# Two experts' rows gathered and transposed at once; own buffers for a mixer's first two weight blocks; the router's block ahead in the queue

## The chip, the core and the metric

One core of a Trainium2 chip. The metric is the device time in microseconds of one execution. The core has TensorE (PE: matmuls and transposes), VectorE (DVE), ScalarE (ACT), GpSimd (POOL) and SyncE (SP), and 16 DMA engines that move data between the chip's memory (HBM) and on-chip memory. The engines run their own instruction streams in order and wait for each other through semaphores.

## What is computed

One sequence of 512 tokens of width 1024, float32, passes through two blocks. The first is a feed-forward network, a mixer with two kinds of attention, and another feed-forward network. The second is a mixer and a layer of experts, one of which each token picks in a hierarchy:

```python
def first_block(x, ...):
    x = x + 0.5 * swiglu(rms_norm(x, g_ffn1), w1_gate, w1_up, w1_down)
    h = rms_norm(x, g_mix)
    proj = h @ w_in
    (c_q, k_a, v_a, k_idx, w_idx, q_b, k_b, v_b, gate_a, gate_b) = jnp.split(proj, offsets, axis=-1)
    ...

def hierarchical_moe(h, w_group, b_group, w_expert, b_expert, w_gate, w_up, w_down):
    # 4 groups of 8 experts: the best group, then the two best experts in it
    ...
    def expert_block(args):
        xb, e = args
        hid = jax.nn.silu(xb @ w_gate[e]) * (xb @ w_up[e])
        return hid @ w_down[e]
    ...
```

Each of the 32 experts has a gate and an up matrix of 1024 x 512 and a down matrix of 512 x 1024, 6 MB together, so 192 MB of expert weights are read once.

## The kernel before

**Planning and queues.** A planner in `build` writes a list of steps in the order in which they shall run, and five programs (`pe_program`, `act_program`, `dve_program`, `pool_program`, `sp_program`) walk through it and issue their engine's part of each step. The order on an engine is the order of the list. SyncE issues all weight loads from one queue, in the order of the units.

**Small units.** Outside the experts a weight block is a `unit` (line 307) of up to 128 x 1024 values. It takes one of 5 stage buffers (`stages`, a ring: a load waits until the matmuls of the unit five before are done) and one of 4 `highs` buffers. ScalarE rounds the block to its high part (wH), VectorE computes the low part in place in the stage buffer (stage0L to stage4L), two units ahead of use, and TensorE multiplies three combinations of high and low. `dense` (line 323) is the step of one block of 8 x 128 rows by 128 columns: 24 matmuls.

**The first mixer.** The first feed-forward network ends with eight down steps (11 chunks of 128 rows each) for each half. Then the mixer (`mixer1`) starts with two dense steps `cq` 0 and 1 on columns 0 to 255 of `w_in`, the row of norm factors, the narrow value blocks (`vw`) and the keys.

**The router and the first experts.** The last six small units are the output projection's columns 3 to 7 of the second half (`w2o`, 12 matmuls each) and the router's block (`w_r`). The router's step, the norm factors, the transposition of all tokens to rows (`turn_xT`), their store to a table in HBM (`store_h`, GpSimd), and `choose` follow, which makes the assignment of tokens to places. Experts 0 and 1 get their tokens by a matmul with a one-hot matrix (`first`); `table` makes the table of token numbers `tok`, and `extras` the numbers `ei` of experts that overflow (with their count).

**The experts.** Blocks of 64 places for each of 32 experts (NB), and up to 15 extra blocks (NX) in conditional regions that run only if an expert overflows. For each expert n the steps are two halves of `project` (gate and up, 16 matmuls of 64 x 512 each), `turn_hid` (4 transposes), `down` (16 matmuls), and for each pair one `spread`, the scatter by a one-hot matmul into 8 token chunks with additions by VectorE. The rows of expert n come by `fetch` (an indirect DMA from GpSimd that gathers 64 rows of 4 KB into `xg`, three buffers, NGR) and `turn_x` (8 transposes of 64 x 64 and one VectorE multiplication by the gain into `xF`, two buffers). The first three fetches wait for `ei`, as their buffers lie where tables of the router's stage were.

**Large buffers.** Expert weights are loaded in units of 1 MB (`weights`), 192 in all, into a ring of 18 buffers of 8 KB a partition. Seven of these are free when the mixer's values are done, the others after steps of the output projection, the router or the norm factors; six lie where the stage and highs buffers and the operand h are. From the 19th load on, each waits for the matmuls that read its buffer's last content.

**The order of loads** at the border is written out in `sp_program` (line 3152): all small units but the last six, two large ones, then six times a small and a large one, then the rest of the large ones.

Of the kernel before, what the change touches and what calls it, by code (L numbers as in the profile page):

```python
# [235 lines left out]
def build(nc, A, out):  # L236
    with contextlib.ExitStack() as ctx:
# [69 lines left out]
        def unit(parts, k, n, until, whole=False):  # L307
# [4 lines left out]
            u.raw = stages.take(until)  # L312
# [10 lines left out]
        def dense(steps, key, parts, K, act, until, ready=None, n=None):  # L323
            s = Step("dense", key=key, K=K, act=act, ready=ready)
            s.unit = unit([(0, parts)], K, 128, ("mm",) + key)
            s.bank = banks.take(until, n)
            steps.append(s)
            return s.bank
# [105 lines left out]
        def mixer1():  # L434
# [25 lines left out]

            M.cq = cq = pair([128, 2, 512], "cq")
            M.cqf, M.ki = sb([128, 2, 512], F32, "cqf"), pair([128, 512], "ki")
# [54 lines left out]
            for m in range(2):  # L517
                bcq.append(dense(steps, ("cq", m), wcols("w_in", m * 128, 128), 8, h, ("cqf", m), "norm" if m == 0 else None, 4 + m))
                steps[-1].gain = "g_mix"
# [730 lines left out]
        NGR = 3  # L1250

        def moe():
# [7 lines left out]
            M.tok = sb([BLK, NB + NX], I32, "tok")  # L1260
# [10 lines left out]
            for k, s in dict(lg=[4, 36], gm=[4], a4=[4, 4], oh=[4, 4], oo=[2, 4, 32], m8=[8, 32],  # L1271
                             v1=[4], v2=[4], gw=[4], vm=[4], ct=[32], nx=[32], cx=[32], on=[32], dx=[32], ps=[4, 32],
                             e8=[8], d8=[8], c8=[8], j8=[8], J=[8, 64]).items():
# [7 lines left out]
            assert place[0] <= rows_at + 4096 * NGR, place[0] - rows_at  # L1281
# [20 lines left out]
            for slot in M.xg.slots:  # L1302
                slot[1] = ("ei",)
            M.xF2 = sb([128, 2, 8, BLK], F32, "xF")
            M.xF = [M.xF2[:, k, :, :] for k in range(2)]
# [30 lines left out]
            def fetch(n):  # L1336
                xg[n] = M.xg.take(("mm", "xT", n))
                add(Step("fetch", n=n, xg=xg[n]))

            def turn_x(n):  # L1340
                add(Step("turn_x", n=n, xg=xg[n], bank=banks.take(("xT", n), 2)))
# [42 lines left out]
            for n in range(2, 2 + NGR):  # L1384
                fetch(n)
# [10 lines left out]
            for n in range(NB):  # L1396
# [13 lines left out]
                if 0 < n < NB - 2:  # L1410
                    turn_x(n + 2)
                if n + 2 + NGR < NB:
                    fetch(n + 2 + NGR)
# [3 lines left out]
                if n == 0:  # L1417
                    turn_x(2)
                if n == 2:
# [39 lines left out]
        def pe_program(pe):  # L1459
# [313 lines left out]
            def expert_steps(steps):  # L1773
                for s in steps:
                    n = s.n
                    if s.kind == "turn_x":
# [6 lines left out]
                    elif s.kind == "project":  # L1783
                        pe.wait_ge(*(after("xT", n) if n >= 2 else after("xT", 0, s.i)))
# [1485 lines left out]
```

## Time and profile before

| | |
|---|---|
| median of 3 runs | 2028.13 us (2027.52 to 2030.19) |
| the profiled execution | 2028.83 us, its span 2027.0 us |
| PE busy | 1924.9 us (95%) |
| DVE, ACT, POOL busy | 1053.2, 704.8, 57.3 us |
| mean granted clock of PE | 0.985 |
| bytes read from HBM | 333.0 MB |
| DMA queue of SyncE | 322.28 MB |
| DMA queue of GpSimd | 15.15 MB |

The span is the stretch between the first and the last instruction of the profiled execution. Busy shares are means over all stages. The span cut into 40 slices shows them: tenths of busy time of each engine, the granted clock of PE, the share of the 16 DMA engines and what they moved.

```profile
PE   7999999997999989999999999999998999999997
DVE  5443544367667886544334446666764333332333
PEclk9999999998999999999999999999998999999999
DMA  6333332333222304333333333222189999999996
```

### The profile page before, as it was taken

The numbers are of one execution on the slowest core, as the hardware profiler recorded it, in microseconds if no ns is written. First come the engines' busy times: TensorE is split into PE (matmuls) and PEld (weight loads), VectorE is DVE, ScalarE is ACT, GpSimd is POOL, SyncE is SP. The second block draws the span as 40 slices with busy tenths as digits, with TensorE's granted clock in tenths as the row PEclk, the third lists the DMA queues.
The fourth block names the chain that finished last, engine by engine and source line by source line (L and its number), as shares of the span: only waits on it lengthen the run. The fifth ranks groups of instructions, "written<-read, shape, count | busy, mean of one in ns | idle before, by whom it ended". The sixth has DMA issues, their size and how long they took to land.

```text
span 2027.0 us, 22190 instructions
## 1 busy us (share of the span) xinstructions
PE 1924.9 (95%) x8902; PEld 1392.4 (69%) x8902; DVE 1053.2 (52%) x1686; ACT 704.8 (35%) x1150; POOL 57.3 (3%) x81
## 2 busy tenths in 40 slices
PE   7999999997999989999999999999998999999997
PEld 6888888775878767888888878877675444444443
DVE  5443544367667886544334446666764333332333
ACT  5321322345545354432222234665652111111111
POOL 0000000100000001000000000000001000000000
PEclk9999999998999999999999999999998999999999
DMA  6333332333222304333333333222189999999996
GB/s 176 95 89 106 96 94 84 71 78 54 70 67 68 109 22 133 95 94 94 94 104 94 94 94 94 76 61 57 32 295 384 406 403 400 406 409 409 409 412 260
DMA packets 260639, 338.92 MB, mean 167 GB/s; under 512 B 10305, under 2 KB 224321, under 8 KB 236977
## 3 DMA queue, kind: packets, MB, share of 16 engines
q1 hardware_dynamic: 254496, 322.28, 46.9%
q0 software_dynamic: 6032, 15.15, 2.2%
q8 instruction: 72, 1.18, 0.2%
q14 instruction: 39, 0.31, 0.0%
HBM read 333.00 MB, written 8.39 MB: 168 GB/s over the span
## 4 chain that ended last, share of the span: by engine, by line
PE 72%; DMA 13%; DVE 9%; ACT 5%; issue 1%; SPq 0%; DVEq 0%; POOLq 0%; ACTq 0%
PE bank L182 70%; DMA large<-w_up 10%; PE bank L185 2%; DMA stage<-w_in 1%; ACT wH L188 1%; ACT p L188 1%; DVE PTL L194 1%; ACT T L188 1%; DVE y L194 1%; DMA xg<-token_rows,tok 1%; DMA stage<-w_r 1%; DVE p L197 1%; DVE score L218 0%; DVE score L200 0%; DVE top L215 0%
## 5 line engine op out<-in xcount | busy, mean ns | idle before, releaser
L182 PE MATMUL bank<-hH,wH 128*128 128x512 f32 x1104 | 438.2, 397 | 21.0 <-DVE stage0L L194 12.0
L182 PE MATMUL bank<-hL,wH 128*128 128x512 f32 x1104 | 431.8, 391 | 0.0
L188 ACT ACTIVATE wH<-stage 128x1024 fp32r<-128x1024 f32 (+3 forms) x238 | 232.5, 987 | 113.0 <-PE bank L182 83.7
L182 PEld LDWEIGHTS bank<-hH,wH 128*128 128x128 f32 x1104 | 209.0, 189 | 68.3 <-DVE stage0L L194 12.0
L182 PE MATMUL bank<-large,xF 128*64 128x512 f32 x1024 | 235.6, 602 | 15.4 <-DMA large<-w_up 14.6
L182 PEld LDWEIGHTS bank<-hL,wH 128*128 128x128 f32 x1104 | 208.9, 189 | 44.3 <-issue 1.9
L182 PEld LDWEIGHTS bank<-large,xF 128*64 128x64 f32 x1024 | 75.0, 138 | 146.4 <-issue 127.8
L182 PE MATMUL bank<-hidH,wH 128*128 128x512 f32 x352 | 137.5, 391 | 2.1 <-DVE stage2L L194 0.9
L182 PE MATMUL bank<-hidL,wH 128*128 128x512 f32 x352 | 137.1, 389 | 0.0
L182 PE MATMUL bank<-large,hF 128*64 128x512 f32 x512 | 116.9, 598 | 1.9 <-DVE hF L194 1.9
L194 DVE TENSOR_TENSOR yoL<-bank,yoH 64x512 fp32r<-64x512 f32 x64 | 44.1, 689 | 110.2 <-ACT yoH L188 109.2
L188 ACT ACTIVATE hidH<-hf 128x512 fp32r<-128x512 f32 x44 | 27.8, 632 | 188.8 <-DVE hf L194 188.8
L188 ACT ACTIVATE yoH<-bank 64x512 fp32r<-64x512 f32 x64 | 37.8, 591 | 157.5 <-PE bank L182 156.7
L200 DVE SCALAR_TENSOR_TENSOR xT<-bank,xT 128x512 f32<-128x512 f32 x32 | 22.1, 691 | 133.4 <-PE bank L182 133.4
L182 PE MATMUL bank<-hH,stage2L 128*128 128x512 f32 x232 | 90.8, 392 | 0.0
L182 PE MATMUL bank<-hH,stage4L 128*128 128x512 f32 x232 | 90.4, 389 | 0.0
L182 PE MATMUL bank<-hH,stage1L 128*128 128x512 f32 x224 | 88.2, 394 | 0.0
L194 DVE TENSOR_TENSOR xt<-bank,xt 128x512 f32<-128x512 f32 x128 | 79.2, 681 | 15.5 <-PE bank L182 15.5
L182 PE MATMUL bank<-hH,stage0L 128*128 128x512 f32 x208 | 81.7, 393 | 0.0
L182 PE MATMUL bank<-hH,stage3L 128*128 128x512 f32 x208 | 81.0, 390 | 0.0
L188 ACT ACTIVATE sg<-sg 128x512 f32<-128x512 f32 x60 | 36.9, 628 | 124.9 <-DVE sg L194 124.8
L182 PEld LDWEIGHTS bank<-hidH,wH 128*128 128x128 f32 x352 | 66.1, 188 | 17.5 <-DVE stage3L L194 1.3
(480 smaller groups left out, 3356.3 us busy)
## 6 DMA issues: line engine op xcount, KB each, us to landing
large<-w_gate SPq DMA_DIRECT2D x64, 1024.0 KB, 26.9
large<-w_up SPq DMA_DIRECT2D x64, 1024.0 KB, 27.8
large<-w_down SPq DMA_DIRECT2D x64, 1024.0 KB, 27.8
stage<-w_in SPq DMA_DIRECT2D x58, 512.0 KB, 4.3
stage<-w_gate SPq DMA_DIRECT2D x44, 512.0 KB, 3.8
stage<-w_up SPq DMA_DIRECT2D x44, 512.0 KB, 3.7
stage<-w_down SPq DMA_DIRECT2D x16, 512.0 KB, 3.8
gates<-gt POOLq DMA_DIRECT2D x16, 256.0 KB, 4.0
```

The source lines that it names most:

```text
L182: return self.e.matmul(*a, **k) if self.e is not None else Nothing()
L185: return self.e.transpose(*a, **k) if self.e is not None else Nothing()
L188: return self.e.activation(*a, **k) if self.e is not None else Nothing()
L194: return self.e.tensor_tensor(*a, **k) if self.e is not None else Nothing()
L197: return self.e.tensor_scalar(*a, **k) if self.e is not None else Nothing()
L200: return self.e.scalar_tensor_tensor(*a, **k) if self.e is not None else Nothing()
```

## The change

Three things:

- **Own buffers for `cq` 0 and 1.** Their raw blocks go into two buffers of 4 KB a partition that lie where the mixer puts `cq` later, and that the first feed-forward network does not use. They take nothing from the ring of stage buffers. `sooner` holds the units before which they are loaded: `cq` 0 ahead of the unit seven before it, `cq` 1 ahead of the unit six places before itself, without a wait.
- **The router's block.** The last six small units are followed by a large one only three times; then come the remaining small ones, the router's the last of them, and then all other large ones. Since the ring of stage buffers is shifted by two, the large buffers that lie over it come free after other steps, and take other places in the ring.
- **Pairs.** `fetch` gathers 128 rows, of experts n and n + 1 (n even), into one of two buffers; `turn_pair` makes 8 transposes of 128 x 128 into two banks (2 and 4) and two VectorE multiplications into `xF2`, two buffers of a pair each. `tok` has the two experts of a pair in the two halves of the partitions, and extra blocks have a table of their own, `tokx`. Only the second buffer of `xg` waits for `ei`. Turning and fetching are done for even n, a pair ahead.

```diff
@@ -304,12 +304,12 @@
-        def unit(parts, k, n, until, whole=False):
+        def unit(parts, k, n, until, whole=False, raw=None):
...
-            u.raw = stages.take(until)
+            u.raw = raw or stages.take(until)
@@ -320,9 +320,9 @@
-        def dense(steps, key, parts, K, act, until, ready=None, n=None):
+        def dense(steps, key, parts, K, act, until, ready=None, n=None, raw=None):
             s = Step("dense", key=key, K=K, act=act, ready=ready)
-            s.unit = unit([(0, parts)], K, 128, ("mm",) + key)
+            s.unit = unit([(0, parts)], K, 128, ("mm",) + key, raw=raw)
@@ -458,7 +458,11 @@
+            at = place[0]
             M.cq = cq = pair([128, 2, 512], "cq")
+            first_raw = [Use([nc.alloc_sbuf_tensor_at(f"cq_weights{m}{part}", [128, 1024], dt, offset=at + 4096 * m) for part, dt in (("", F32), ("L", F32R))], None, NSTAGE + m)
+                         for m in range(2)]
+            M.sooner = {}
@@ -515,7 +519,8 @@
-                bcq.append(dense(steps, ("cq", m), wcols("w_in", m * 128, 128), 8, h, ("cqf", m), "norm" if m == 0 else None, 4 + m))
+                bcq.append(dense(steps, ("cq", m), wcols("w_in", m * 128, 128), 8, h, ("cqf", m), "norm" if m == 0 else None, 4 + m, first_raw[m]))
+                M.sooner[steps[-1].unit.i + m - 7] = steps[-1].unit
@@ -1247,7 +1252,7 @@
-        NGR = 3
+        NGR = 2
@@ -1257,7 +1262,7 @@
-            M.tok = sb([BLK, NB + NX], I32, "tok")
+            M.tok, M.tokx = sb([128, NB // 2], I32, "tok"), sb([BLK, NX], I32, "tokx")
@@ -1269,8 +1274,8 @@
-                             v1=[4], v2=[4], gw=[4], vm=[4], ct=[32], nx=[32], cx=[32], on=[32], dx=[32], ps=[4, 32],
-                             e8=[8], d8=[8], c8=[8], j8=[8], J=[8, 64]).items():
+                             v1=[4], v2=[4], gw=[4], vm=[4], ct=[32], nx=[32], on=[32], dx=[32], ps=[4, 32],
+                             e8=[8], d8=[8], c8=[8], j8=[8], J=[8, 64], cx=[32]).items():
@@ -1278,7 +1283,7 @@
-            assert place[0] <= rows_at + 4096 * NGR, place[0] - rows_at
+            assert place[0] <= rows_at + 4096 * NGR + 4096
@@ -1299,10 +1304,11 @@
-            for slot in M.xg.slots:
-                slot[1] = ("ei",)
-            M.xF2 = sb([128, 2, 8, BLK], F32, "xF")
-            M.xF = [M.xF2[:, k, :, :] for k in range(2)]
+            M.xg.slots[1][1] = ("ei",)
+
+            late_xF = sb([128, 2, 8, BLK], F32, "xF")
+            M.xF2 = [sb([128, 2, 8, BLK], F32, "xF"), late_xF]
+            M.xF = [M.xF2[k][:, e, :, :] for k in range(2) for e in range(2)]
@@ -1334,11 +1340,15 @@
-                xg[n] = M.xg.take(("mm", "xT", n))
+
+                xg[n] = M.xg.take(("mm", "xT", n, 1) if n < NB else ("mm", "xT", n))
...
-                add(Step("turn_x", n=n, xg=xg[n], bank=banks.take(("xT", n), 2)))
+                if n < NB:
+                    add(Step("turn_pair", n=n, xg=xg[n], banks=[banks.take(("xT", n, c), at) for c, at in enumerate((2, 4))]))
+                else:
+                    add(Step("turn_x", n=n, xg=xg[n], bank=banks.take(("xT", n), 2)))
@@ -1381,8 +1391,8 @@
-            for n in range(2, 2 + NGR):
-                fetch(n)
+            for p in range(1, 1 + NGR):
+                fetch(2 * p)
@@ -1407,15 +1417,16 @@
-                if 0 < n < NB - 2:
+                if n % 2 == 0 and 0 < n < NB - 2:
                     turn_x(n + 2)
-                if n + 2 + NGR < NB:
-                    fetch(n + 2 + NGR)
+                    if n + 2 + 2 * NGR < NB:
+                        fetch(n + 2 + 2 * NGR)
...
+                    fetch(2 + 2 * NGR)
@@ -1773,7 +1784,15 @@
-                    if s.kind == "turn_x":
+                    if s.kind == "turn_pair":
+                        pe.wait_ge(*after("xg%d" % s.xg.at, n))
+                        rows = s.xg.t[:, :].rearrange("s (c p k) -> s c p k", c=2, k=4)
+                        for c in range(2):
+                            free(s.banks[c])
+                            for k in range(4):
+                                t = pe.transpose(s.banks[c].t[:, 128 * k:128 * k + 128], rows[:, c, :, k], mat("ident"))
+                            t.then_inc(*did("mm", "xT", n, c))
+                    elif s.kind == "turn_x":
@@ -1781,14 +1800,14 @@
-                        pe.wait_ge(*(after("xT", n) if n >= 2 else after("xT", 0, s.i)))
+                        pe.wait_ge(*(after("xT", n) if n >= NB else after("xT", n - n % 2, s.i)))
...
-                                t = pe.matmul(s.bank.t[BLK * j2:BLK * j2 + BLK, :], xF[n % 2][:, 4 * s.i + j, :], u.F[:, j, :],
+                                t = pe.matmul(s.bank.t[BLK * j2:BLK * j2 + BLK, :], xF[n % 4][:, 4 * s.i + j, :], u.F[:, j, :],
@@ -2354,7 +2373,7 @@
-                                t = act.activation(M.xF2[:, :, 4 * c + k, :], s.banks[c].t[:, 128 * k:128 * k + 128].rearrange("p (e n) -> p e n", e=2),
+                                t = act.activation(M.xF2[0][:, :, 4 * c + k, :], s.banks[c].t[:, 128 * k:128 * k + 128].rearrange("p (e n) -> p e n", e=2),
@@ -2933,7 +2952,9 @@
-                then(dve.tensor_copy(M.tok[:, :], tf), "tok")
+                for half in range(2):
+                    then(dve.tensor_copy(M.tok[BLK * half:BLK * half + BLK, :], tf[:, half:NB:2]), *([] if half == 0 else ["tok"]))
+                then(dve.tensor_copy(M.tokx[:, :], tf[:, NB:]), "tokx")
@@ -2951,11 +2972,20 @@
-                    if s.kind == "turn_x":
+                    if s.kind == "turn_pair":
+                        dve.wait_ge(*after("gain_in", 7))
+                        if n >= 4:
+                            dve.wait_ge(*after("mm", "gu", n - 3, 1, 1))
+                        for c in range(2):
+                            dve.wait_ge(*after("mm", "xT", n, c))
+                            dve.tensor_tensor(M3.xF2[n // 2 % 2][:, :, 4 * c:4 * c + 4, :].rearrange("p e k n -> p k e n"),
+                                              s.banks[c].t[:, :].rearrange("p (k e n) -> p k e n", k=4, e=2),
+                                              gain2[:, 4 * c:4 * c + 4].unsqueeze(2).unsqueeze(3).broadcast_to([128, 4, 2, BLK]), ALU.mult).then_inc(*did("xT", n, c))
+                    elif s.kind == "turn_x":
...
-                        dve.tensor_tensor(xF[n % 2], s.bank.t[:, :].rearrange("p (k n) -> p k n", k=8), wide(gain2[:, :], [128, 8, BLK]), ALU.mult).then_inc(*did("xT", n))
+                        dve.tensor_tensor(xF[n % 4], s.bank.t[:, :].rearrange("p (k n) -> p k n", k=8), wide(gain2[:, :], [128, 8, BLK]), ALU.mult).then_inc(*did("xT", n))
@@ -3075,12 +3105,13 @@
-                        pool.wait_ge(*after("tok",))
+                        K, ids = (128, M3.tok[:, n // 2:n // 2 + 1]) if n < NB else (BLK, M3.tokx[:, n - NB:n - NB + 1])
+                        pool.wait_ge(*after("tok" if n < NB else "tokx",))
...
-                        pool.indirect_dma_start(out=s.xg.t[0:BLK, :], out_offset=None, in_=h_rows[:, :],
-                                                in_offset=bass.IndirectOffsetOnAxis(ap=M3.tok[:, n:n + 1], axis=0),
+                        pool.indirect_dma_start(out=s.xg.t[0:K, :], out_offset=None, in_=h_rows[:, :],
+                                                in_offset=bass.IndirectOffsetOnAxis(ap=ids, axis=0),
@@ -3149,13 +3180,16 @@
-            small, big = [[u for u in units[4:M3.main] if (u.size > CAP) == k] for k in (False, True)]
+            small, big = [[u for u in units[4:M3.main] if (u.size > CAP) == k and u not in M1.sooner.values()] for k in (False, True)]
             for u in small[:-6] + big[0:2]:
+                if u.i in M1.sooner:
+                    load(M1.sooner[u.i])
...
-                load(big[2 + k])
-            for u in big[8:]:
+                if k < 3:
+                    load(big[2 + k])
+            for u in big[5:]:
...

```

## Rows read from the trace of the kernel before

**Rows 1.** busy time by stage: PE, PEld, DVE, ACT, POOL busy (count); clock, DMA, GB/s

```profile
1600.00:1960.00 360.00, 347.94 (x1647) 154.41 (x1648) 124.04 (x206) 54.05 (x96) 25.13 (x24) 1.00 1.01 406
1960.00:1998.00 38.00, 35.49 (x167) 15.62 (x164) 11.62 (x19) 5.69 (x10) 0.00 (x0) 1.00 1.01 420
```

**Rows 2.** the chain that ended last, experts: start, us, what

```profile
1742.57 1.10 PE bank L185 x8
...
1771.25 1.10 PE bank L185 x8
...
1777.72 27.58 DMA large<-w_up
1805.44 2.85 PE bank L182 x13
...
1992.74 5.70 PE bank L182 x24
```

**Rows 3.** timeline of PE, first mixer: start, us, instruction, idle before it

```profile
385.12 0.79 PE L182 MATMUL bank<-hH,wH 128*128 128x512 f32 x1 [3.16 <-DVE stage2L L194]
...
392.05 1.02 PE L182 MATMUL bank<-acc,mats 128*128 128x512 f32 x2
```

**Rows 4.** SyncE's queue at the end of the first network: start, us, loads

```profile
309.56 0.37 SPq L224 DMA_DIRECT2D stage<-w_down  x1
...
322.48 0.92 SPq L224 DMA_DIRECT2D stage<-w_down  x2
...
361.09 0.99 SPq L224 DMA_DIRECT2D stage<-w_in  x2
```

**Rows 5.** timeline of ACT, around the same loads

```profile
333.05 1.04 ACT L188 ACTIVATE wH<-stage 128x1024 fp32r<-128x1024 f32 x1
...
340.53 1.99 ACT L188 ACTIVATE wH<-stage 128x1024 fp32r<-128x1024 f32 x2
...
377.92 0.62 ACT L188 ACTIVATE xsq<-xT 128x512 f32<-128x512 f32 x1
382.75 1.38 ACT L188 ACTIVATE wH<-stage 128x1024 fp32r<-128x1024 f32 x2 [4.22 <-DMA stage<-w_in]
```

**Rows 6.** all 58 loads of the two w_in arrays: issue to landing

```profile
DMA to landing us min/median/max: 3.6/4.3/21.2
```

**Rows 7.** SyncE's queue, from the first large block on

```profile
1480.49 0.37 SPq L224 DMA_DIRECT2D large<-w_gate  x1
...
1498.14 2.17 SPq L224 DMA_DIRECT2D stage<-w_r  x1
...
1519.51 0.43 SPq L224 DMA_DIRECT2D large<-w_up  x1
1539.63 0.33 SPq L224 DMA_DIRECT2D large<-w_gate  x1
```

**Rows 8.** busy time by stage: first mixer, and the first 85 us of large loads

```profile
385.00:392.00 7.00, 6.88 (x24) 5.61 (x25) 1.65 (x3) 0.77 (x1) 0.00 (x0) 0.78 0.02 3
1480.00:1499.00 19.00, 19.00 (x86) 15.44 (x85) 12.93 (x21) 10.44 (x18) 0.00 (x0) 1.00 0.99 335
1480.00:1540.00 60.00, 53.81 (x290) 44.05 (x289) 42.91 (x98) 26.43 (x52) 2.69 (x5) 0.97 1.02 383
1540.00:1550.00 10.00, 10.00 (x55) 6.32 (x55) 3.12 (x12) 1.59 (x2) 2.89 (x3) 1.00 0.98 366
1550.00:1565.00 15.00, 12.62 (x52) 4.47 (x50) 2.49 (x4) 2.63 (x5) 0.93 (x1) 0.79 1.02 345
```

**Rows 9.** timeline of PE, output projection, router, first gathered rows

```profile
1506.47 0.50 PE L182 MATMUL bank<-haH,wH 128*128 128x512 f32 x1 [0.55 <-DVE stage1L L194]
...
1511.95 0.50 PE L182 MATMUL bank<-hH,wH 128*128 128x512 f32 x1 [2.42 <-DVE stage2L L194]
...
1557.63 1.17 PE L185 MATMUL bank<-mats,xg 64*128 64x64 f32 x8 [1.55 <-DMA xg<-token_rows,tok]
```

**Rows 10.** timeline of DVE, last instruction ahead of the mixer's second block

```profile
378.71 0.68 DVE L194 TENSOR_TENSOR acc<-acc,xsq 128x512 f32<-128x512 f32 x1
```

## The prediction, made before the changed kernel ran

> **What bounds the kernel now.** I read four views in this order: the busy time by stage, the chain that ended last, the queue of SyncE (which issues every weight load), and the timelines of single engines around the three places that the change touches.
>
> The busy time by stage says that the last quarter is the DMA's. From 1600 to 1960 us the 16 DMA engines are busy at a share of 1.01 and move 406 GB/s, with 24 row gathers among the expert weights; from 1960 to 1998, with no gather, 420 GB/s [rows 1]. TensorE is busy in nearly all of the same time, so the share alone does not tell who sets the pace. The chain does. Until 1771 a pair of experts takes 1771.25 - 1742.57 = 28.7 us, which is TensorE working off blocks that landed earlier; from 1805 to 1992 six pairs take 1992.74 - 1805.44 = 187.3 us, 31.2 us each, and each ends on the landing of an up block, as the one issued at 1777.72 that landed 27.6 us later [rows 2]. A pair's twelve blocks of 1 MB at 406 GB/s take 12.58 / 0.406 = 31.0 us: the DMA's pace is the longer one, TensorE used up its stock by 1777, and what it saves before that only makes it wait sooner. So the end is: the moment at which the first large block is issued (1480.49 [rows 7]), plus the time the stream needs, plus the tail after the last wait (2027.0 - 1992.7 = 34.3 us), which the change does not touch. What comes ahead of 1480 counts in full, since nothing there goes by an absolute time; what comes behind counts only where it keeps the stream full.
>
> **Part 1, own buffers for the mixer's first two blocks.** Both blocks are issued together at 361.09, because both take a stage buffer that the same down step frees [rows 4]. Usual landing of such a block is 4.3 us, the longest of all 58 is 21.2 us [rows 6]; it is this one, for ScalarE is held 4.22 us by it and splits it only at 382.75 [rows 5], and TensorE starts the second block at 385.12 after 3.16 us of idleness [rows 3]. Its 24 matmuls then take until 392.05, 6.93 us, since the granted clock is 0.78 on average over 385 to 392 [rows 8], part of it at 1.2 GHz after the idle time. At the full clock 86 matmuls fill 19.00 us [rows 8], 0.221 us each, so 24 take 5.3 us. With the block there in time, idleness and slow clock both go: 3.16 + 6.93 - 5.30 = 4.8 us. What is late next? ScalarE is free at 377.92 + 0.62 = 378.5 and needs 1.0 us for the split; VectorE is free at 379.4 [rows 10] and needs 1.2 us for its half, so the block is ready near 380.9, and TensorE reaches it at 385.12 - 3.16 = 382.0. A margin of 1 us; the whole 4.8 us is kept, and everything after it moves forward.
>
> What the early loads cost: they go out right behind the down loads of 309.56 and of 322.48 [rows 4], without a wait, and SyncE loses 0.4 us each. The loads behind them may land late, as the first reads of this array were slow at 361. By the longest landing the first is down by 331, and the down block behind it is wanted by ScalarE at about 333; the second by 345, while the block behind it is wanted at 340.5 to 341.5 (two splits at 333.05 and 340.53, of 1.0 us a block [rows 5]) and by TensorE only some 8 us later. Bounds 0 to 2 us; I take 0, as two loads that follow each other alone have shorter landings than two at once. From there the ring of five stage buffers skips two takes, so the next five loads (the narrow value and key blocks) go out one or two down steps earlier; they were hidden before and stay so. The highs ring, and with it the order of the splits, is unchanged.
>
> **Part 2, the router's block sooner.** It is the last of six small loads. Before, a large block follows each; now only the first three. Its issue at 1498.14 [rows 7] hung mostly on its stage buffer: it was issued at once behind a large block whose own issue took 1.8 us, and the buffer came free near 1497.8, so its issue moves by some 0.4 us only. But two large blocks (2.1 MB, 5.7 us at some 365 GB/s) no longer lie ahead of it in the queues. TensorE's idle 0.55 us at 1506.5 and 2.42 us at 1512, both for weights [rows 9], go; the router and all that follows on TensorE, VectorE and ScalarE come 3.0 us sooner. The other side: blocks 5 and 6 of the stream are issued after 1497.8 and not between the small loads. Is the stream then dry? Issued by 1497.8 are five large and five small blocks, 5.24 + 1.31 = 6.55 MB; moved from 1480 to 1499 are 19 x 335 = 6.37 MB [rows 8]. It comes within 0.2 MB of dry. Cost between 0 and 1.5 us, taken 0.3.
>
> Do the 3.0 us reach the end? Only through the stream. All 18 large buffers are filled by 1519.51, and the next load waits until 1539.63 for the first projection of expert 0 to free one [rows 7]. By then 18 x 1.049 MB of weights, 1.8 MB of small blocks, 0.3 MB of constants and 2.1 MB of token rows have been issued, 23.1 MB, and 60 x 383 = 23.0 MB moved [rows 8]: the stream is dry at that moment, and the next 10 us run at 366 GB/s. With the release 3.0 us earlier it does not run dry. Worth at most 10 x (406 - 366) / 406 = 1.0 us there, and up to 15 x (406 - 345) / 406 = 2.3 us from 1550 to 1565 [rows 8], where I blame the first three gathers more than missing work. I take 1.0 us of the 3.3.
>
> **Part 3, gathers and transposes by pairs.** Fifteen gathers of 128 rows take the place of 30 of 64: same rows, same bytes. For a pair TensorE transposes 8 times instead of 16 (eight take 1.10 us [rows 2]), VectorE keeps two scalings, and the index table costs it two small copies more. TensorE saves 0 to 1.1 us a pair, at nothing in the sum, because the stream sets the pace; if it did not, this would be the gain of rival B. The pair's transposition waits for bank 4, which VectorE frees in the second half of the scatter, and behind it on TensorE stands the down projection; TensorE has 2.5 us a pair to spare for that. On GpSimd a gather now waits for the transposition two pairs back, still a pair ahead of its use. The first gather no longer waits for the extra experts' numbers; before, TensorE lost 1.55 us on it at 1557.6 [rows 9] and a stretch of slow clock. Worth up to some 5 us to TensorE, again only through the stream, and in the 2.3 us above.
>
> What a gather costs the stream is the unknown. 406 against 420 GB/s over 360 us is 12 us for 24 gathers, 0.5 us each. If that goes with the instruction, half of it goes: 6.7 us over 27 gathers. If it goes with the rows, nothing. With three gathers close together (1540 to 1565) the loss is at most 3.3 us, 1.1 each, so bunching them did not make them cheaper; I take 0.
>
> The Trainium skill (DMA: Bandwidth & Descriptors, section Anatomy of one DMA — SWDGE (gpsimd) path) gives each software DMA a fixed part of about 2.0 us. Were that time of the DMA engines, 13 gathers fewer would save 26 us, an estimate by that page; the 0.5 us above speaks against it, and the page itself calls it mostly completion latency.
>
> **The sum.** -4.8 - 1.0 + 0.3 = -5.5 us. The profiled execution took 2028.8 us with a span of 2027.0; its span would be 2021.5. From the median of the runs shown, 2028.13, it gives 2022.6 us.
>
> **The rivals.** A is the forecast.
>
> B, the gathers' cost goes with the instruction: another 6.7 us, 2016 us. For it: the rate does rise when gathers stop. Against: bunched gathers cost no less.
>
> C, the first part brings nothing: the slow reads only move into the first network's down projection, or another late operand (the margin was 1 us) or clock drops that fall otherwise take the 4.8 us. Then 2027.4 us, or 2026 with half of it. For it: the granted clock falls in other stretches too (0.79 over 1550 to 1565 [rows 8]), and such stretches can move.
>
> D, slower: a gather of 128 rows counts as two bunched ones, 2 x 1.1 = 2.2 us against 2 x 0.5 = 1.0 in two single ones. 1.2 us more for 13 pairs is 15.6 us: 2038 us. It decides from 9.6 / 13 = 0.7 us a pair on. For it: 345 GB/s with three in flight. Against: those were also the first reads of the table of rows, and part of that loss was the dry stream.
>
> **Chances.** A 0.63, B 0.12, C 0.19, D 0.06. A measurement of this kernel can tell about 0.2% (4.1 us) from no change. A's own range is 2020.5 to 2025, mostly beyond that bound: 0.53 of its 0.63 counts as faster. With B and a little of C, faster is 0.67; same is the rest of A and C, 0.28; slower 0.05. The range from 2017 to 2027.5 takes in half of B and nearly all of C, and leaves D out.
>
> **What would show it.** TensorE without idleness between the mixer's first two blocks, clock 1.0 there, and the first large block issued near 1475.7. The router's matmuls with no wait for weights, and large blocks whose issue stands still for no more than 20 us before expert 0 frees one. From 1600 on a rate of 406 GB/s if gathers cost by rows, 412 or more under B, below 395 under D. TensorE waiting for up blocks sooner than 1777. The prediction is wrong if the gap from the first large issue to the last wait differs from 1992.7 - 1480.5 = 512 us by more than 2 us.

## The result, and the profile after

The changed kernel takes 2008.93 us (median of 4 runs, 2008.36 to 2010.52) against 2028.45 us of the kernel before beside it (4 runs, 2027.52 to 2030.19): a ratio of 0.9895, 95% interval 0.9881 to 0.9909, 19.5 us less. Forecast were 2022.6 us and a range of 2017.0 to 2027.5. The direction was right, the size was not: 5.5 us forecast, 19.5 measured.

The profiled execution of the changed kernel has a span of 2008.6 us, 18.4 less than before. The chain that ended last, in the expert stage (start, us, what), answers to [rows 2]:

```profile
1790.95 28.29 DMA large<-w_up
1819.38 3.42 PE bank L182 x15
1822.80 27.95 DMA large<-w_up
1850.88 7.25 PE bank L182 x24
...
1945.17 26.38 DMA large<-w_up
1971.69 5.72 PE bank L182 x24
```

It has the same form: TensorE waits for up blocks, from 1758.34 on where the kernel before had its first such wait at 1805.44, and the last one ends at 1945.17 + 26.38 = 1971.55. But a pair of experts takes (1971.69 - 1850.88) / 4 = 30.2 us, where it took 31.2. SyncE's queue (start, us, loads) shows the first large block, the wait for the first buffer that expert 0 frees, and the second buffer's load, as in [rows 7]:

```profile
1478.02 0.37 SPq L224 DMA_DIRECT2D large<-w_gate  x1
...
1495.35 0.37 SPq L224 DMA_DIRECT2D stage<-w_r  x1
...
1513.52 0.43 SPq L224 DMA_DIRECT2D large<-w_up  x1
1535.05 0.33 SPq L224 DMA_DIRECT2D large<-w_gate  x1
```

The span splits at that first issue. What lies ahead of it became 1480.5 - 1478.0 = 2.5 us shorter. From there to the last wait, a stretch called the stream below, it took 1971.55 - 1478.02 = 493.5 us against 1992.61 - 1480.49 = 512.1: 18.6 us less. The tail behind the last wait takes 37.0 us against 34.4, and gives 2.7 us back; over all fourteen profiles of this case the tail is between 34.4 and 38.4 us long, so this too is scatter as far as the profiles show. So nearly the whole difference lies in the stream, where 0.7 us were forecast.

Busy time by stage (window, length; busy us and count of PE, PEld, DVE, ACT, POOL; clock, DMA share, GB/s) answers to [rows 1] and [rows 8]:

```profile
385.00:392.00 7.00, 7.00 (x43) 5.88 (x42) 0.00 (x0) 2.60 (x3) 0.00 (x0) 1.00 0.00 0
1540.00:1550.00 10.00, 10.00 (x48) 4.40 (x46) 1.25 (x5) 3.04 (x4) 1.01 (x1) 1.00 1.01 413
1550.00:1565.00 15.00, 13.32 (x66) 5.15 (x64) 3.49 (x6) 2.25 (x4) 0.99 (x1) 1.00 1.01 420
1600.00:1900.00 300.00, 288.45 (x1336) 125.34 (x1334) 107.90 (x182) 46.91 (x83) 10.87 (x11) 0.99 1.01 420
1970.00:1980.00 10.00, 8.31 (x38) 4.09 (x40) 3.02 (x6) 0.94 (x2) 0.00 (x0) 1.00 0.98 406
1980.00:1990.00 10.00, 8.05 (x38) 3.53 (x36) 5.77 (x10) 2.25 (x4) 0.00 (x0) 1.00 0.34 141
```

The DMA moves 420 GB/s with 11 gathers on the way, the rate that the kernel before reached only without gathers. Neither is there a slow stretch after 1540.

The other two places. In the timeline of PE the mixer's second block follows the first without idle time and at full clock, and the norm matmul starts at 388.21 instead of 392.05 [rows 3]; ScalarE splits the block at 379.20, ahead of need [rows 5]. The first block starts at 377.12 here and at 376.36 before; from there to the norm matmul it takes 11.1 us against 15.7, so 4.6 us are gained in place. That start in the timeline of PE of the kernel before, then timelines of PE and of ACT of the changed kernel:

```profile
376.36 0.39 PE L182 MATMUL bank<-hH,wH 128*128 128x512 f32 x1
```

```profile
377.12 0.39 PE L182 MATMUL bank<-hH,wH 128*128 128x512 f32 x1
...
387.99 0.39 PE L182 MATMUL bank<-hH,cq_weights1L 128*128 128x512 f32 x1
388.21 1.02 PE L182 MATMUL bank<-acc,mats 128*128 128x512 f32 x2
```

```profile
379.20 1.04 ACT L188 ACTIVATE wH<-cq_weights 128x1024 fp32r<-128x1024 f32 x1
```

At the router TensorE's two waits for weights [rows 9] are down to one of 0.21 us, and the first matmul behind the router starts 1512.01 - 1478.02 = 34.0 us after the first large issue; before it was 1517.52 - 1480.49 = 37.0. For the first pair TensorE does not wait for the gathered rows, but 1.68 us for their scaling:

```profile
1500.97 0.50 PE L182 MATMUL bank<-haH,wH 128*128 128x512 f32 x1 [0.21 <-DVE stage3L L194]
...
1512.01 0.95 PE L182 MATMUL bank<-mats,acc 128*128 128x1 f32 x8
...
1554.34 3.65 PE L182 MATMUL bank<-large,xF 128*64 128x512 f32 x16 [1.68 <-DVE xF L194]
```

### The profile page after: what moved, and what is told of

Its sections match the earlier page's. It is cut to its first block, busy times and chain, and to the rows that moved or that the text cites. A ratio compares the mean times of both kernels' runs of the same rounds, so it can differ in the third digit from the quotient of the medians.

```text
span 2008.6 us, 21936 instructions
## 1 busy us (share of the span) xinstructions
PE 1908.5 (95%) x8782; PEld 1382.1 (69%) x8782; DVE 1051.0 (52%) x1688; ACT 704.1 (35%) x1150; POOL 41.1 (2%) x66
## 4 chain that ended last, share of the span: by engine, by line
PE 75%; DMA 9%; DVE 9%; ACT 5%; issue 1%; SPq 1%; DVEq 0%; ACTq 0%
PE bank L182 74%; DMA large<-w_up 8%; PE bank L185 1%; ACT p L188 1%; ACT wH L188 1%; DVE y L194 1%; DVE PTL L194 1%; SPq L224 1%; DVE p L197 0%; DVE score L200 0%; DMA stage<-w_out 0%; DVE st L206 0%; DMA stage<-w_gate 0%; DVE cv L200 0%; ACT T L188 0%
## 5 line engine op out<-in xcount | busy, mean ns | idle before, releaser
L182 PE MATMUL bank<-hH,stage0L 128*128 128x512 f32 x232 | 91.3, 394 | 0.0
L182 PE MATMUL bank<-hH,stage4L 128*128 128x512 f32 x216 | 85.3, 395 | 0.0
L182 PEld LDWEIGHTS bank<-large,hF 128*64 128x64 f32 x512 | 36.3, 138 | 68.8 <-issue 63.5
L194 DVE TENSOR_TENSOR hF<-sgT,bank 128x256 f32<-128x256 f32 x32 | 13.5, 421 | 132.1 <-ACT sgT L188 132.1
L182 PE MATMUL bank<-hH,stage1L 128*128 128x512 f32 x208 | 81.0, 390 | 0.0
```

The lines of the kernel that those rows point to most:

```text
L182: return self.e.matmul(*a, **k) if self.e is not None else Nothing()
L194: return self.e.tensor_tensor(*a, **k) if self.e is not None else Nothing()
```

## The experiments

Each was timed beside the kernel before on the same chip. There the medians of the kernel before were 2030.4 to 2031.5 us with a scatter of some 10 us, so the ratios are known to within 0.1 to 0.3% either way. The stream, read from one profile each, is steadier: the changed kernel's was 493.5 and 493.2 us in two profiles. But own buffers, which should not touch the stream, changed it by 0.4 us (own_only against before) and by 1.0 us (pairs_and_own against pairs_only), so differences of about 1 us mean nothing.

| kernel | median | ratio to before, interval | stream, us | GB/s, 1600 to 1900 |
|---|---|---|---|---|
| before | | | 512.1 | 406 |
| own_only | 2027.18 | 0.9979, 0.9966 to 0.9993 | 512.5 | 406 |
| router_only | 2027.83 | 0.9980, 0.9968 to 0.9992 | 508.0 | 406 |
| pairs_only | 2015.03 | 0.9923, 0.9898 to 0.9947 | 495.7 | 420 |
| pairs_and_own | 2012.05 | 0.9904, 0.9883 to 0.9924 | 496.8 | 420 |
| changed_again | 2011.44 | 0.9903, 0.9884 to 0.9922 | 493.2 | 420 |
| wide_gather | 2027.73 | 0.9984, 0.9970 to 0.9998 | 507.5 | 418 |
| two_wide | 2010.04 | 0.9890, 0.9871 to 0.9909 | 495.6 | 419 |
| two_halves | 2027.58 | 0.9981, 0.9970 to 0.9993 | 511.6 | 404 |
| after_lumped | 2013.79 | 0.9920, 0.9903 to 0.9937 | 499.5 | 420 |
| after_mixed | 2009.64 | 0.9904, 0.9888 to 0.9921 | 492.7 | 420 |
| before_mixed | 2039.67 | 1.0051, 1.0034 to 1.0067 | 519.5 | 403 |
| before_checker | 2033.40 | 1.0019, 1.0005 to 1.0033 | 513.8 | 403 |

### One part at a time

**own_only.** The kernel before with the two `cq_weights` buffers and their early loads, nothing else.

> Only the own buffers of the mixer's first two blocks on the kernel before. The prediction said 4.8 us at 388 us, all of it kept. In the changed kernel 3.8 us are seen at 388 and 2.5 at 1478. Theory 1, all is kept: 4 to 5 us faster. Theory 2, later waits of the mixer take part of it: 2 to 3 us faster. The rate in the expert stage stays at 406 GB/s by both.

Measured: a ratio of 0.9979, 1.4 to 6.9 us less. The first large block is issued at 1475.53. In the eight profiles with own buffers it is issued at 1474.7 to 1480.3 us, on average at 1476.6, in the six without at 1479.7 to 1482.2, on average at 1480.9: 4.3 us sooner, with a scatter of 1 to 2 us from one execution to another. By the time of a run alone theory 1 (4 to 5 us) and theory 2 (2 to 3) can't be told apart; the means speak for theory 1, and the 2.5 us of the first comparison lie within that scatter.

**router_only.** The order of loads alone:

```diff
             for k, u in enumerate(small[-6:]):
                 load(u)
-                load(big[2 + k])
-            for u in big[8:]:
+                if k < 3:
+                    load(big[2 + k])
+            for u in big[5:]:
                 load(u)
```

> Only the order of loads at the router on the kernel before. By the prediction's account (stream dry at 1540, dryness worth 1.0 us, cost of the new order 0.3): 0.7 us faster. Rival: the slow stretch from 1540 to 1565 (366 and 345 GB/s) is the gathers' and not dryness; then the rates there stay and the time is within 0.5 us of before. The router's matmuls start 2 to 3 us sooner after the first large load by both.

Measured: the stream is 4.1 us shorter, and the ratio of 0.9980 says 1.6 to 6.5 us: more than either account expected. From 60 to 70 us after the first large issue it moves 390 GB/s where the kernel before moves 363, in the next 15 us 368 against 342, then 407 against 402. In the first 20 us, where the new order could cost something, it moves 337 against 339, which is next to nothing. The slow stretch was in part a dry stream.

**pairs_only.** All of the pair part, without own buffers and with the old order.

> Only the pair part of the change (gathers of 128 rows, transposes of two experts) on the kernel before. The changed kernel moves 420 GB/s in the expert stage where the one before moved 406. Theory 1, the whole of that comes from the gathers by pairs: this kernel moves 420 GB/s from about 1545 us on and is 14 to 16 us faster than the kernel before. Theory 2, the stream runs faster because it is not dry at 1540 (the router's part): this kernel stays at 406 GB/s and is within 3 us of the kernel before.

Measured: the stream is 16.4 us shorter. Its busy time by stage:

```profile
1540.00:1550.00 10.00, 10.00 (x57) 6.60 (x54) 3.45 (x14) 0.69 (x1) 2.07 (x2) 1.00 0.87 325
1550.00:1565.00 15.00, 13.32 (x65) 5.20 (x66) 3.38 (x6) 3.93 (x6) 0.99 (x1) 1.00 1.01 421
1600.00:1900.00 300.00, 288.56 (x1344) 127.29 (x1342) 107.79 (x182) 46.17 (x82) 10.88 (x11) 0.99 1.01 420
```

The two causes of the slow stretch part here. Around 1545 the engines are busy only 0.87 of the time: the stream is dry, as the buffers come no sooner than before. From 1550 on, where the kernel before moved 345 GB/s, it is 421: that loss belonged to the gathers.

**pairs_and_own.** The changed kernel with the old order of loads.

> The changed kernel with the old order of loads at the router: what is the order worth once the gathers are paired? By the difference of the stretches measured (495.7 with the pairs alone, 493.5 in the changed kernel) 2.2 us; alone it was 4.1 us. Theory 1, it fills the dry moment 60 us after the first large load: 318 to 325 GB/s there instead of 415, and 2 to 3 us slower than the changed kernel. Rival, the order itself does nothing and the stretches differ by chance: the same time and rate as the changed kernel.

Measured: 496.8 us, 3.2 to 3.5 longer than the changed kernel, with the dry moment back (317 GB/s from 60 to 70 us after the first large issue, share 0.87; 415 in the changed kernel). The router's order works through the dry stream, with 2.2 to 4.1 us in three comparisons. The time itself, 2012.05 us, can't be told from the changed kernel's.

**changed_again.** The changed kernel once more.

> The changed kernel once more, beside before_checker and the kernel before, for its first large issue and its stretch: 1475 to 1478 us and 493 to 495 us. Were the 1478.0 us of its first profile not chance but what the own buffers are worth together with the other parts, it would be 1477.5 to 1478.5 again.

Measured: a ratio of 0.9903, a stream of 493.2 us and 420 GB/s, as in the first comparison. Its first large issue stands at 1480.31, later than either range that was expected, where the first profile of the same kernel had 1478.02: the scatter lies ahead of the stream.

### What the gathers cost: number, shape or balance

**wide_gather.** The kernel before, each gather with 128 places, the upper 64 out of bounds:

```diff
-            M.tok = sb([BLK, NB + NX], I32, "tok")
+            M.tok = sb([128, NB + NX], I32, "tok")
...
-                then(dve.tensor_copy(M.tok[:, :], tf), "tok")
+                then(dve.memset(M.tok[BLK:128, :], 1024))
+                then(dve.tensor_copy(M.tok[0:BLK, :], tf), "tok")
...
-                        pool.indirect_dma_start(out=s.xg.t[0:BLK, :], out_offset=None, in_=h_rows[:, :],
+                        pool.indirect_dma_start(out=s.xg.t[:, :], out_offset=None, in_=h_rows[:, :],
```

> The kernel before, but each of its 30 gathers names 128 rows, the upper 64 of them out of bounds, so that they write nothing: as many gathers and as many rows moved as before, only the shape of the transfer is that of the changed kernel. Theory N, the stream pays for each gather instruction: 406 GB/s, time as before. Theory S, it pays for the shape of a transfer to 64 partitions: 415 to 420 GB/s from 1600 to 1960 and 10 to 15 us faster. Theory I, the rows in use lie on half of the DMA engines and those are late: 406 GB/s or less, as all rows in use still lie in the lower 64 partitions.

Measured: no theory fits by itself. The rate is that of theory S, 418 GB/s with 30 gathers, but the stream is only 4.6 us shorter. The end of its stream tells why (the last line is its last 5 us):

```profile
1600.00:1900.00 300.00, 293.02 (x1388) 129.33 (x1386) 104.68 (x174) 46.27 (x82) 23.14 (x21) 1.00 1.01 418
1970.00:1980.00 10.00, 10.00 (x49) 4.51 (x48) 4.55 (x7) 1.78 (x3) 0.00 (x0) 1.00 1.01 424
1980.00:1990.00 10.00, 9.14 (x46) 3.86 (x48) 1.91 (x4) 2.07 (x4) 0.00 (x0) 1.00 0.80 330
1984.68:1989.68 5.00, 4.27 (x22) 1.60 (x21) 1.17 (x3) 1.02 (x3) 0.00 (x0) 1.00 0.61 256
```

The last wait ends at 1989.68, but in the 5 us ahead of it only 0.61 of the engines' time is in use. I read this as some engines being through while others still move the blocks for which TensorE waits. The packet records agree: 191.2 MB of weights have been moved by the last wait, where the kernels whose engines stay busy to the end have moved 188.0 to 188.9. The kernel before has a share of 1.01 in its last 5 us. A mean rate over 16 engines is not the pace of the stream if one of them is behind.

**two_wide.** The changed kernel with twice as many gathers of its shape, the second of a pair issued when the first has landed:

```diff
+                        if n < NB:
+                            for half, table in enumerate((M3.tok, M3.tokb)):
+                                if half:
+                                    pool.wait_ge(*after("xg%d" % s.xg.at, "first", n))
+                                pool.indirect_dma_start(out=s.xg.t[:, :], out_offset=None, in_=h_rows[:, :],
+                                                        in_offset=bass.IndirectOffsetOnAxis(ap=table[:, n // 2:n // 2 + 1], axis=0),
...
```

> The changed kernel, but each pair is gathered in two gathers of 128 rows, one with the upper and one with the lower 64 places out of bounds, the second after the first has landed: as many gathers as before the change, shape and balance of the changed kernel. Measured so far from the first large issue to the last wait for a weight block: 512.1 us before, 507.5 with wide gathers, 495.7 with the pairs alone, 493.5 in the changed kernel, 499.5 with its places lumped on half of the engines. Theory N (each gather, with its skipped rows, costs the stream 0.4 us): 499 to 500 us here. Theory I alone (only the most loaded engine counts): 493 to 494.

Measured: 495.6 us, 2.1 to 2.4 longer than the changed kernel, between the two theories. The number of gathers is worth at most about that much, skipped places included: some 0.15 us for each of the 15 more, read from a difference of about twice the scatter of the stream.

**two_halves.** The same number, each gather with the 64 partitions of one expert (by two index tables of 64 rows each):

```diff
+                            for half in range(2):
+                                at = slice(BLK * half, BLK * half + BLK)
+                                pool.indirect_dma_start(out=s.xg.t[at, :], out_offset=None, in_=h_rows[:, :],
+                                                        in_offset=bass.IndirectOffsetOnAxis(ap=(M3.tok, M3.tokb)[half][:, n // 2:n // 2 + 1], axis=0),
...
```

> The changed kernel, but each pair is gathered in two gathers of 64 rows, the first to partitions 0 to 63, the second to partitions 64 to 127. Theory S (a gather to 64 partitions disturbs the weight stream): the rate falls back to 404 to 408 GB/s and the stretch from first large issue to last wait is 506 to 512 us, nearly all of the pairs' gain gone though the transposes stay paired. Theory N alone: the same as two_wide within 2 us, at 417 to 420 GB/s.

Measured: 511.6 us and 404 GB/s, the values of the kernel before. Everything else of the pairs is in this kernel, the paired transposes, the early first fetch, the order of loads and the own buffers. 16 us separate it from two_wide, which has as many gathers, the same rows and the same buffers:

```profile
1600.00:1900.00 300.00, 275.10 (x1252) 117.94 (x1250) 98.91 (x167) 44.71 (x79) 18.71 (x20) 0.98 1.01 404
```

One thing more sets these two apart: in two_wide the second gather waits for the first, in two_halves both can be under way at once. wide_gather and the kernel before do not differ in that, and their rates part in the same way, 418 against 406 GB/s. So the gain of the pairs is that a gather spans 128 partitions and no longer 64.

A kernel whose gathers move no row at all (before_no_rows) was to give the price of the bare instruction. It has no time: its experts compute on stale rows, and these held non-finite numbers. That price rests on two_wide alone.

**after_lumped.** The changed kernel with the places of an expert in another order, so that the 32 or so rows in use lie on partitions 0 to 15 and 32 to 47 of its half (the comparisons with `iota` that make the one-hot places are written in two parts, in the order 0 to 15, 32 to 47, 16 to 31, 48 to 63).

> The changed kernel, with the places of an expert reordered the bad way: places 0 to 15 on partitions 0 to 15 and places 16 to 31 on partitions 32 to 47. The gathers are the 15 of the changed kernel, 128 rows each. Theory I, with engines that serve partitions 4k to 4k+3 and 32+4k to 35+4k: 8 of 16 engines carry 8 rows a pair each, as in the kernel before: pairs of 30.8 to 31.1 us instead of 30.2, 8 to 13 us slower than the changed kernel, that is some 8 us faster than before. Theories N and S: nothing changes, as fast as the changed kernel.

Measured: 499.5 us, 6.0 to 6.3 longer than the changed kernel. Theory I expected 8 to 13; the direction is right, the size is below it. The rate is still 420 until 1900, and the uneven end is there again, in the 5 us ahead of the last wait at 1974.63, with 190.5 MB of weights moved by then; the changed kernel has a share of 1.00 in its last 5 us (third line):

```profile
1600.00:1900.00 300.00, 284.36 (x1311) 123.72 (x1311) 104.37 (x176) 45.25 (x81) 10.87 (x11) 0.98 1.01 420
1969.63:1974.63 5.00, 2.83 (x14) 0.72 (x10) 1.38 (x2) 1.33 (x3) 0.00 (x0) 1.00 0.87 362
1966.55:1971.55 5.00, 2.77 (x14) 0.72 (x10) 1.38 (x2) 1.28 (x3) 0.00 (x0) 1.00 1.00 418
```

Where on the partitions the rows in use lie decides how long the stream takes, and the uneven end says that it does so by how evenly the DMA engines are loaded. The Trainium skill (DMA: Bandwidth & Descriptors, section The descriptor swizzle) says that a transfer of 128 partitions is split so that one engine writes four partitions and the four that lie 32 above them, eight engines for the lower 64 and eight for the upper. after_lumped was built on that map, and the 6 us agree: under a map of eight partitions that follow each other, or one by the remainder by 16, the old and the new order would load the engines alike. In wide_gather, by the same map, all rows lie on eight engines. Its stream is then accounted for to 1 to 4 us: 493.5, and 6.0 to 6.3 for the lumped rows, 2.1 to 2.4 for 15 more gathers and 2.2 to 4.1 for the old order of loads make 503.8 to 506.3 of 507.5 us.

**after_mixed.** The other way: places b, 16+b, 32+b, 48+b on each group of four partitions.

> The changed kernel with the places mixed as in before_mixed. With 32 tokens an expert the load of the engines is the same as in the changed kernel; with experts of 40 and more tokens it is more even. Theory I: 0 to 2 us faster than the changed kernel. N and S: the same time.

Measured: 492.7 us, 0.5 to 0.8 shorter, and a ratio of 0.9904 like the changed kernel's. Not to be told from it.

**before_mixed.** The same order in the kernel before, with gathers of 64.

> The kernel before, with its 30 gathers of 64 rows, but the 64 places of an expert lie in another order on the partitions: every group of four partitions holds places b, 16+b, 32+b and 48+b instead of four that follow each other. An expert has about 32 tokens, so before, the rows in use lay on partitions 0 to 31 and a row out of use moves 4 bytes. Theory I (each DMA engine serves four partitions that follow each other, so half of the engines carry all gathered rows and the stream waits for them): 4 rows a pair and engine instead of 8 on the loaded half, 4 x 0.16 = 0.6 us less a pair; pairs take 30.4 to 30.7 us instead of 31.2, and the kernel is 8 to 12 us faster. Theories N (each gather instruction costs) and S (the shape of 64 partitions costs): pairs of 31.2 us, the time within 2 us of before.

Measured: the opposite of theory I. It is slower, by a ratio of 1.0051, and the stream 7.4 us longer. Either the 64 rows are not dealt to the engines in groups of four, or rows above partition 32 cost more. Its last 5 us speak for the first: the engines are unevenly loaded, where the kernel before has a share of 1.01, and 190.5 MB of weights have been moved by the last wait, against 188.9 there.

```profile
1994.60:1999.60 5.00, 2.73 (x14) 0.71 (x10) 1.65 (x3) 1.18 (x2) 0.00 (x0) 1.00 0.87 364
```

**before_checker.** A third order for the kernel before, even by groups of four, by the remainder by 16, and between the partitions below and above 32 (four comparisons instead of one, by the parity of the partition).

> The kernel before with a third order of places: the 32 rows in use of an expert lie on every second partition of each 16, even ones and odd ones in turns. That is two in every group of four that follow each other, two for every remainder by 16, and as many above partition 32 as below. before_mixed, with two in every group of four but rows in use on 8 of 16 remainders only, stretched the stream to 519.5 us from 512.1. Theory R, a gather to 64 partitions deals its rows to the 16 DMA engines by the remainder of the partition by 16, so before_mixed loaded half of the engines: 511 to 513 us here, the time of before. Theory G, it deals them by groups of four, and before_mixed lost because half of its rows lay on partitions 32 to 63: 518 to 521 us here, some 8 us slower than before.

Measured: 513.8 us, 1.7 more than before and 5.7 less than before_mixed, and the share in its last 5 us is back at 1.00. Since as many rows lie above partition 32 here as in before_mixed, their place above 32 is not what cost the 5.7 us. That is nearer to theory R (a gather of 64 deals its rows by the remainder by 16), just outside its numbers; that the rows are dealt so is inferred from these orders and not seen.

The trace also has a record for each DMA packet. Between some 1610 and 1950 us, the weight packets of 8 KB and the gathered rows of 4 KB (`after` is the changed kernel):

```
                 weights  over    mean | gathered  mean
                          350 ns  ns   | rows      ns
before           16517    1125    323  |   663     204
wide_gather      16955      84    315  |   668     162
two_halves       16471    1261    324  |   628     207
before_mixed     16435    1612    325  |   634     198
before_checker   16415    1533    325  |   634     204
pairs_only       17097      16    314  |   635     163
two_wide         17052      16    314  |   635     164
after            17097      16    314  |   635     163
```

With gathers of 64 partitions one weight packet in 10 to 15 takes over 350 ns and a row takes 200 ns; with 128 there are nearly none, and a row takes 163. The disturbance is mutual, and it goes with the shape: wide_gather and two_wide have as many gathers and do not show it. It accounts for the loss: 9 ns on each of 16517 weight packets and 41 ns on each of 663 rows, over 16 engines, are 11 us of these 340, and 14 GB/s of 420 are 11 us too. Why a transfer to 64 partitions gets in the way of the weights stays open, as the records do not name the engine of a packet.

## Why the prediction was wrong, point by point

**The bound: right.** The stream of weights sets the end of the expert stage. TensorE saved work there (8 transposes for 16) and only waited sooner, from 1758 on and not from 1805. One sign failed: I wrote that the issue of large blocks would stand still for no more than 20 us before expert 0 frees a buffer. It stood still from 1513.95 to 1535.05, 21.1 us, and the stream was not dry: 415 GB/s from 60 to 70 us after the first large issue.

**Part 1: right.** 4.8 us forecast, 4.3 us by the means of the first large issue, 1.4 to 6.9 by own_only's time, and 4.6 in place. The missing 0.2 us is a reading: 86 matmuls in 19.00 us gave 0.221 us each, but they follow each other every 0.23 us here. The early loads held up nothing that the profile shows; the two blocks land after 11.2 and 12.3 us where the slower one took 21.2 [rows 6], hidden behind the down steps. Rival C falls (with half of part 1 it would have been 2025.0 us, not 2026).

**Part 2: mechanism right, term too small.** The 3.0 us on TensorE came exactly, and the reasoning that they count only through the dry stream held. I put its worth at 1.0 us of a bound of 3.3, and 0.3 us of cost against it. It was 4.1 us alone and 2.2 to 3.5 us together with the pairs, and the cost was not to be seen.

**Part 3: here the forecast failed.** The step is "same rows, same bytes", and with it "if it goes with the instruction, half of it goes; if it goes with the rows, nothing". The size of the loss was read rightly, 406 against 420 GB/s, 12 us over 360 us [rows 1]. But I asked only what half as many gathers would save, never whether the new gather is a different transfer. It is: 128 partitions instead of 64, and the whole loss went, 16.4 us in pairs_only, of which some 2 are the number (two_wide) and the rest is shape. That gathers close together did not get cheaper [rows 8] spoke against a price for each instruction, and rightly; it said nothing of the shape. So rival B reached no further than 2016 and the range ended at 2017; the measured time lay 7 us below the one and 8 below the other. Rival D, the opposite, took 345 GB/s with three gathers in flight for their bunching; in pairs_only, with the stream dry before it, the same stretch ran at 421.

The balance of the engines was neither in the forecast nor in its rivals. That the changed kernel profits from it is luck of its layout: the rows in use lie on partitions 0 to 31 and 64 to 95, and after_lumped shows 6 us that could have been lost.

**The 2.0 us of a software DMA** that the Trainium skill gives (DMA: Bandwidth & Descriptors, section Anatomy of one DMA — SWDGE (gpsimd) path) would, taken as engine time, have given 26 us for 13 fewer gathers, an estimate by that page; by two_wide, 15 more cost 2.1 to 2.4 us in all. As engine time it does not hold here.

## What to carry to other kernels

Where a stream of large transfers sets the pace, price a small transfer by what the stream loses with it, and ask of every change to it three things apart: how many instructions, over how many partitions, and on which partitions its bytes lie. In this kernel gathers that span all 128 partitions were the better ones, with the rows in use on both halves of them. And compare the mean rate with the length of the stream: when the one rises and the other does not fall, look at the last few us of the stream for a share of busy DMA engines below 1.

## What the hardware showed that I had not expected

- A gather of 64 rows to 64 partitions slows the weight stream by 3.3% (406 against 420 GB/s) while moving 2% of its bytes; the same rows in gathers of 128 partitions cost nothing beyond their bytes (420 GB/s with and without them).
- Weight packets of 8 KB take 313 ns as a rule; beside gathers to 64 partitions one in 10 to 15 took over 350 ns.
- With the loads uneven (after_lumped) the mean rate still reads 420 GB/s for 400 us, while 2 MB more of weights have been moved by the last wait; the loss of 6 us shows as a lower share only in the last 5 us (0.87).
- The first two blocks of `w_in` landed late wherever they were put: after 10.1 and 21.2 us when they were read together, after 11.2 and 12.3 when one followed the other, and the loads of `w_in` from 1200 us on after 3.9 us in the median. In the first mixer later blocks too took up to 15.1 us (before) and 13.8 (changed), so being first is not shown as the cause.
